# Three rounded passes for the fp32 input projection of a hybrid decoder step

## The reference, cut to what matters

```python
proj = xn @ w_in                       # 1024 -> 3*1024 + 1024 + 1536 + 16 columns
q, k, v, z, xbc, dt_raw = split(proj)
attn = rmsnorm(attend(rope(q), rope(k), v), g_attn)
xbc = silu(causal_conv(xbc))           # 4 taps
y, h = ssd_scan(x, dt, a, B, C, h0)    # h = h*exp(a*dt) + dt*x*B ;  y = C.h
y = rms(( y + d_skip*x) * silu(z)) * g_ssd
out = concat(attn, y) @ w_out          # then a PEER expert mixer
```

## Time and profile before

| | |
|---|---|
| device time, 3 runs | 1175.99, 1178.31, 1179.5 us |
| profiled execution: span | 1177.8 us (no other time of this execution is shown) |
| TensorE matmul busy | 1145.5 us, 97% |
| VectorE / ScalarE / GpSimd busy | 67% / 48% / 64% |
| mean granted TensorE clock | 0.994 of full speed |

### The profile page before, as it was taken

How to read it: one execution, slowest core, us unless ns; L and a number is a source line. 1 busy time by engine, 2 the same in 40 slices (tenths; PEclk the granted TensorE clock), 3 DMA queues, 4 the chain that set the end, 5 groups by cost and what they waited for, 6 DMA issues and landing times.

```text
span 1177.8 us, 24286 instructions
## 1 busy us (share of the span) xinstructions
PE 1145.5 (97%) x7599; PEld 1012.2 (86%) x7599; DVE 793.4 (67%) x1718; ACT 569.8 (48%) x1289; POOL 758.9 (64%) x642
## 2 busy tenths in 40 slices
PE   8999999989999999999999999999999999999997
PEld 7887777758888999999999999998888887888876
DVE  6789788874299997002899999984454466665534
ACT  3323223544354555565555554445555555555545
POOL 0066443237355998988666666676677797789754
PEclk9999999999999999999999999999999999999999
DMA  7468667695443666656544455545666697788653
GB/s 249 143 231 280 195 194 221 207 344 175 152 155 109 199 186 185 187 172 189 143 144 139 141 143 144 144 143 153 187 188 189 189 325 252 224 281 291 191 153 108
DMA packets 108667, 225.13 MB, mean 191 GB/s; under 512 B 12754, under 2 KB 21570, under 8 KB 108074
## 3 DMA queue, kind: packets, MB, share of 16 engines
q1 hardware_dynamic: 104706, 210.50, 57.5%
q0 software_dynamic: 2944, 10.49, 2.6%
q10 hardware_dynamic: 936, 3.14, 0.7%
HBM read 215.80 MB, written 8.19 MB: 190 GB/s over the span
## 4 chain that ended last, share of the span: by engine, by line
PE 71%; issue 1%; DVE 1%; POOL 0%; ACT 0%; DVEq 0%; POOLq 0%; ACTq 0%
PE bank L1689 31%; PE bank L1719 30%; PE bank L1699 5%; PE bank L1642 2%; PE bank L1654 1%; PE bank L1666 1%; DVE hl L2092 0%; PE bank L1739 0%; PE bank L1756 0%; POOL hl L1582 0%; DVE acts L2115 0%; PE bank L1747 0%; ACT acts L1925 0%; POOL hl L1567 0%; PE bank L1774 0%
## 5 line engine op out<-in xcount | busy, mean ns | idle before, releaser
L1567 POOL TENSOR_TENSOR hl<-ring,hl 128x512 fp32r<-128x512 f32 x448 | 585.5, 1317 | 187.5 <-ACT hl L1805 180.5
L1805 ACT CAST hl<-ring 128x512 fp32r<-128x512 f32 x512 | 317.1, 620 | 292.1 <-PE bank L1719 161.7
L1689 PE MATMUL bank<-split,hl 128*128 128x256 f32 x3072 | 378.5, 282 | 0.4 <-ACT hl L1805 0.3
L1689 PEld LDWEIGHTS bank<-split,hl 128*128 128x128 f32 x3072 | 366.3, 189 | 0.8 <-issue 0.5
L1719 PE MATMUL bank<-hl,split 128*128 128x512 f32 x1524 | 353.9, 394 | 1.9 <-DVE hl L2092 1.9
L1719 PEld LDWEIGHTS bank<-hl,split 128*128 128x128 f32 x1524 | 286.2, 188 | 69.7 <-DVE hl L2092 2.4
L533 PE MATMUL pj<-xn,ring 128*128 128x264 f32 x672 | 158.5, 392 | 0.7 <-ACT proj L824 0.7
L2085 DVE TENSOR_TENSOR split<-acts,split 128x256 fp32r<-128x256 f32 x128 | 128.3, 1028 | 40.0 <-ACT split L1901 37.0
L533 PEld LDWEIGHTS pj<-xn,ring 128*128 128x128 f32 x672 | 126.4, 192 | 24.7 <-issue 4.6
L2092 DVE TENSOR_TENSOR hl<-ring,hl 128x512 fp32r<-128x512 f32 x64 | 49.9, 779 | 115.6 <-ACT hl L1805 115.6
L2051 DVE TENSOR_SCALAR bv<-bkey,ig 128x130 f32<-128x130 f32 x256 | 86.0, 394 | 0.0
(11 more groups left out here) (369 smaller groups left out, 1107.1 us busy)
## 6 DMA issues: line engine op xcount, KB each, us to landing
ring<-in_uv SPq DMA_DIRECT2D x256, 256.0 KB, 2.7
ring<-in_v_rows SPq DMA_DIRECT2D x256, 256.0 KB, 3.1
ring<-in_w_ring SPq DMA_DIRECT2D x76, 512.0 KB, 4.2
room<-in_cache_k SPq DMA_DIRECT2D x64, 128.0 KB, 2.8
hs<-in_state_ssm SPq DMA_DIRECT2D x8, 512.0 KB, 4.7
out_ssm_s<-hs SPq DMA_DIRECT2D x8, 512.0 KB, 6.3
acts<-x_rows SPq DMA_DIRECT2D x8, 512.0 KB, 4.7
room<-in_cache_v SPq DMA_DIRECT2D x12, 256.0 KB, 5.7
```

Source lines behind the costliest of these rows:

```text
L1567: nc.gpsimd.tensor_tensor(hl[:, r % HL, 1], raw[:, r], hl[:, r % HL, 0].bitcast(F32), ALU.subtract).then_inc(lo_done, 1)
L1689: mm = nc.tensor.matmul(out, hl[:, r % HL, m, k * P:(k + 1) * P], split[:, x, kk, 0:TP], start=(kk == 0 and n == 0), stop=(kk == KD - 1 an ...
L1805: nc.scalar.copy(hl[:, r % HL, 0], raw[:, r]).then_inc(hi_done, 1)
```

## The change

Tiles 2 to 43 are computed in three passes of fp32r, like the output projection. For each half tile ScalarE rounds the weights into `wi` (`in_high`, right behind `copy(i-2)` in its queue), GpSimd writes the rest over the raw half in the ring (`in_low`), and TensorE runs 24 matmuls. `xn` is split once into `x_high` (ScalarE) and `x_low` (VectorE, which writes over `xn`). The room for `wi` and `x_high` comes from the state slots, which go from four to two, and some small tiles that move. From VectorE the first tap of tiles 4 to 11 (`tap`) and the scaling of the probabilities (`normal`) go to ScalarE; from GpSimd the decay of the state goes to ScalarE (`decay_state`, eight instructions of 128x128 per round). GpSimd's squares now start behind the last `in_low`; `values(0)` is issued in round 7 between two of its steps; `values(1)` moves to a later place of SyncE's queue, and its home from `hs` to the room of `x_high`. Waits on `hs_out` in the output stage become waits on `pj_copied`.

```diff
-HS, NS = 4, 6
+HS, NS = 2, 6
+HOMES = 4
@@ SyncE
-                    if n == 1:
-                        sp.wait_ge(ys_done, KD - 1)
-                        for s in (1, 2):
-                            sp.wait_ge(hs_out[s], 16 * (KD // HS))
-                    elif n == 2:
+                    if n in (1, 2):
                         sp.wait_ge(pj_copied, N_IN)
...
+                        if n == 0 and c >= HS:
+                            state(c)
-                        if n == 3 and 2 <= c < KD - HS + 2:
-                            state(c - 2 + HS)
...
-                            values(1)
...
                 tile(N_IN)
+                values(1)
                 values(2)
@@ GpSimd
+                def in_low(i):
+                    for a in range(2):
+                        n, r = 2 * (i - 2) + a, 2 * (i % RING) + a
+                        pool.wait_ge(w_hi, n + 1)
+                        nc.gpsimd.tensor_tensor(ring_lo[:, r], raw_o[:, r], wi[:, n % HL].bitcast(F32), ALU.subtract).then_inc(w_lo, 1)
+                for i in range(2, CONV_CH):
+                    in_low(i)
...
+                for c in range(KD):
+                    s, g = c % HS, c * GROUPS // KD
+                    in_low(CONV_CH + 4 * c)
...
+                    fed_in.then_inc(fed, 1)
+                    in_low(CONV_CH + 4 * c + 1)
+                    if c == KD - 1:
+                        values(0)
+                    pool.wait_ge(decayed, c + 1)
...
+                    sums.then_inc(st_done, 1)
+                    in_low(CONV_CH + 4 * c + 2)
+                    in_low(CONV_CH + 4 * c + 3)
@@ TensorE
+                    pe.wait_ge(pj_copied, i - 1)
+                    order = [(a, kind) for a in range(2) for kind in range(3)] if i > 2 else [(0, 0), (0, 2), (1, 0), (1, 2), (0, 1), (1, 1)]
+                    for n, (a, kind) in enumerate(order):
+                        half = 2 * (i - 2) + a
+                        if i == 2:
+                            pe.wait_ge(x_los if kind == 1 else x_his, a + 1)
+                        pe.wait_ge(w_lo if kind == 2 else w_hi, half + 1)
+                        for k in range(4):
+                            w = ring_lo[:, 2 * s + a, k * P:(k + 1) * P] if kind == 2 else wi[:, half % HL, k * P:(k + 1) * P]
+                            mm = nc.tensor.matmul(pj[i % 2][:, 0:NT], w, (x_low if kind == 1 else x_high)[:, 4 * a + k],
+                                                  start=(n == 0 and k == 0), stop=(n == 5 and k == 3))
@@ ScalarE
+                def in_high(i):
+                    act.wait_ge(ring_full[i % RING], 16 * (i // RING) + 16)
+                    for a in range(2):
+                        nc.scalar.copy(wi[:, (2 * (i - 2) + a) % HL], raw_o[:, 2 * (i % RING) + a]).then_inc(w_hi, 1)
+                in_high(2)
+                in_high(3)
+                def tap(i):
+                    act.wait_ge(pj_copied, i + 1)
+                    act.wait_ge(silu_done, i - 1)
+                    c = CT[i]
+                    nc.scalar.activation(cv[:, i % 2], proj[:, c, 0:TP], ACT.Copy, scale=par[:, P_CW + c * CONV_W + 3:P_CW + c * CONV_W + 4]
+                                         ).then_inc(tapped, 1)
                 def copy(i):
...
+                    if i + 2 < N_IN:
+                        in_high(i + 2)
...
+                for a in range(2):
+                    act.wait_ge(normed, a + 1)
+                    nc.scalar.copy(x_high[:, 4 * a:4 * a + 4], xn[:, 4 * a:4 * a + 4]).then_inc(x_his, 1)
                 copied_early(1)
...
+                def decay_state(c):
+                    s = c % HS
+                    act.wait_ge(hs_full[s], 16 * (c // HS) + 16)
+                    act.wait_ge(dds_done, 1)
+                    for b in range(NB):
+                        ins = nc.scalar.activation(hs[:, s, b], hs[:, s, b], ACT.Copy, scale=dds[:, c, 0, b:b + 1])
+                    ins.then_inc(decayed, 1)
+                def normal(c):
+                    for j in range(2):
+                        act.wait_ge(recips_done, 2 * c + j + 1)
+                        nc.scalar.activation(sc[:, j, 0:P], sc[:, j, 0:P], ACT.Copy, scale=stat[:, j, 4:5])
+                        nc.scalar.activation(sc[:, j, P:3 * P], sc[:, j, P:3 * P], ACT.Copy, scale=stat[:, j, 5:6]).then_inc(p_ready, 1)
...
                     copy(CONV_CH + 4 * c)
+                    if c:
+                        normal(c - 1)
                     decays(c)
...
                     copy(CONV_CH + 4 * c + 3)
+                    if c < KD - 1:
+                        decay_state(c + 1)
@@ VectorE
-                    link(nc.vector.tensor_scalar(to, proj[:, c, 0:TP], cw[3], None, ALU.mult))
+                    if i < 4:
+                        link(nc.vector.tensor_scalar(to, proj[:, c, 0:TP], cw[3], None, ALU.mult))
+                    else:
+                        dve.wait_ge(tapped, i - 3)
...
+                for half in range(2):
+                    k = slice(half * KD // 2, (half + 1) * KD // 2)
+                    dve.wait_ge(x_his, half + 1)
+                    nc.vector.tensor_tensor(x_low[:, k], xn[:, k], x_high[:, k].bitcast(F32), ALU.subtract).then_inc(x_los, 1)
                 conv(0)
```

111 lines of the change are left out of this document (55 added, 56 removed).

## The result

The changed kernel takes 1199.94 us (median of 4 runs, 1197.86 to 1202.91), the kernel before 1177.25 beside it. The ratio is 1.0201 [1.0173, 1.0229]: slower, by about 2%, outside the predicted range and beside the rival in which the memory port sets the pace (1200). The profiled span is 1201.1 us, 23.3 more than before; it belongs to the slowest of the four runs.

A forecast was written before the change was run, and what follows sets the result against it. TensorE was taken as the bound on average, with waits already costing 1.42 us a round. Rounds -11.6, opening +4.3, round 7 +2, output +2.5, clock +1 sum to -1.8: 1176.5 us, own range 1170 to 1183, full range 1162 to 1197.

The forecast's parts named there:

- The step that failed: Rounds 1 to 7: VectorE's waits grow to 5.7 us a round, about 18.4 us busy, within a 19.6 us round.
- the other two terms: The clock, +1 us, and the rest of the span from the first PEER matmul on, 0.
- The port rival: Rounds: VectorE and GpSimd never overlap on SBUF, a round needs 22.1 us; +22, 1200 us in all; chance 0.30.
- Its opening term (+7): Opening and round 0 in the case where the port sets the pace: 7 us later.
- TensorE's 0.65 us a tile: The 42 tiles: three passes start 2.92 us apart instead of 3.57, 27.3 us in all if everything else keeps up.
- The softmax chain: Rounds: ScalarE's scaling makes TensorE wait about 1.8 us at `turn_probs`; total waits 2.4 us a round instead of 1.42.
- Opening and round 0: Start to end of round 0: tile 5 and VectorE about 5 us late; +4.3 us, bounds +1 and +9.
- Round 7: `values(0)`'s four DMA issues, 4.6 us between GpSimd's steps, hold TensorE for about half: +2 us, between 0 and 4.
- Output stage: Its start: squares and `values(3)` issued later, value unit 3 to 7 us late; +2.5 us, between 0 and 5.
- State loads: Rounds: they wait longer for their slots but are issued a round ahead of the decay; no cost.
- Clock: Opening: more waits make one more half-speed stretch likely; +1 us, 0 to 4.

The follow-up runs named there:

- e16: e13's fp32 kernel plus 48 useless GpSimd subtractions in rounds 1 to 6, results read by nobody: 1178.94 us, 1.0027.
- e5: Changed kernel with GpSimd making only one of each tile's two low halves, used for both (a different computation): 1184.97 us, 1.0065.
- e18: e13's fp32 kernel plus 48 useless GpSimd subtractions and 48 useless ScalarE casts in rounds 1 to 6: 1180.02 us, 1.0037.
- e11: e10 with tiles 2 to 15 left in fp32, x split at the end of round 0, ScalarE copying tile 12 earlier: 1183.34 us, 1.0060.
- e2: Changed kernel with six useless fp32 matmuls on TensorE ahead of `turn_probs` in each round: 1198.43 us, 1.0197.
- e13: e11 with all tiles in fp32, no split of xn and no low weights, the smaller parts of the change kept: 1175.71 us, 1.0000.
- e1: Changed kernel with VectorE's softmax reciprocals ahead of `sample_out`: 1204.78 us, 1.0260.
- e4: Changed kernel with `evict_early(1)` ahead of the split of x and `conv(0)`, and `copy(3)` ahead of the exponentials: 1199.18 us, 1.0186.
- e3: Changed kernel with tile 13's low halves made before GpSimd's wait for `xdt`, tile 14's ahead of the state's sum: 1199.59 us, 1.0205.
- e8: Changed kernel with `values(0)` issued behind the last `in_low`, and `values(2)` ahead of `values(1)` on SyncE: 1202.30 us, 1.0208.
- e10: Changed kernel with `values(0)` and `values(3)` issued behind the last `in_low`, before the squares; SyncE's order unchanged: 1197.55 us, 1.0189.
- e7: Changed kernel with VectorE's order in a round made reciprocals, `ssd_in`, then `sample_out`: 1217.98 us, 1.0344.
- e9: Changed kernel with e7's order and SyncE's load of the next state issued two tiles later: 1225.19 us, 1.0423.
- e12: e11 with the order of e9 in the rounds: 1210.25 us, 1.0289.

## Why the prediction was wrong

**The step that failed** is "The waits grow with GpSimd's work: 114 us in seven rounds times 0.35 is 40 us, 5.7 a round, so about 18.4 us", taken to fit in a round of 19.6. The 0.35 was a mean over rounds in which GpSimd was idle for more than half of the time, taken as a price of added work. The first stretch of the earlier trace rows already spoke for more: (21.90 - 13.95) / (21.97 - 2.92) = 0.42 in a full round. Added work costs 0.52 to 0.55 (e16) and work taken out gives back 0.68 to 0.70 (e5). GpSimd's work came out longer too, 121 us for 114. VectorE was busy (141.15 - 4.4) / 7 = 19.5 us a round, and it has to wait 1.4 us for matmuls of its own chain: 20.9 us. Rounds 2 to 6 took 21.2. I had compared a busy time with a round's length as though it could be filled to the last, and gave nothing for those 1.4 us, which fall mostly on the rounds with key units.

In size, rounds 1 to 6 are 6.7 us of the 25.1 by which the sum missed the span. The largest part is the opening with round 0 (12.0 us), then round 7 (5.0) and the output stage (3.8); the other two terms missed by 2.3 the other way.

**The port rival had the mechanism and the total.** Its own sum for a round, 22.1 us "if no two overlap", is too high as a mean; the runs show about 21, and "whatever TensorE does" doesn't hold: rounds without key units take 20.4 us with fp32 tiles (e18) and 19.3 with three passes (e11). Its opening term (+7) was too small. That its total agrees with the measurement is partly chance: +5.9 for the seven rounds was +2.0 (-3.3 + 5.3).
The Trainium skill ("SBUF — State Buffer", SBUF: two separate sides) has a lock on a shared port pair, held for a whole instruction. The trace agrees on the turns: in round 0 four short instructions of VectorE took 3.66 us beside an unbroken row of GpSimd's. The rule gives neither the 0.52 nor the 5.04 us behind six instructions.

**TensorE's 0.65 us a tile** was right where nothing waits (2.90 us a tile), and the kernel could use it only in the rounds without key units: e2 shows that TensorE has spare time in rounds 2 to 6, and e18 against e11 that over five rounds the shorter tiles are worth nothing. In the kernel before, 5.6 us of rounds 2 to 6 were mostly TensorE's waits on VectorE and ScalarE, and e13 gets them (105.8 to 100.2) by the small moves alone. In the change these moves hid a part of the loss.

**The softmax chain.** Forecast was a wait of 1.8 us at `turn_probs`; it was 1.8 us (11.0 / 6). The reading of it, as the chain that decides, was wrong: e1 takes the wait away and e2 fills it, and neither gains more than 2 us.

**Opening and round 0**: +4.3 forecast (a choice; no sum leads from the 5 us to it), bounds +1 to +9, +16.3 measured. Two terms of it. Up to `expand(0)` +6.0, near the 5 us forecast for VectorE's arrears: tile 5 came at 39.70 (38 forecast), and the split of x took 4.57 us where I had 2.4 plus turns. The seven tiles' gain of 4.6 us didn't come, as VectorE's convolutions set the pace (a reading of the timeline; e4 agrees). Then round 0 lost 10.3 us for which the forecast had nothing ("round 0's own gain goes into waits on it"). Two things were missed. GpSimd waits 4.65 us for `xdt` with `in_low` of the next tiles behind it in its queue; I had not asked what stands behind that wait. And it then works without a pause from 77.56 on, just beside VectorE's chain to the last rope, which takes 18.0 us for 10.4: 7.6 of the 10.3 us. The chain's later start behind `expand(0)` is 3.2 more. e3 shows that the wait alone is not the cause. e5, with half of the low work, gives back 10.1 of the 16.4 us by the end of round 0; that the rest lies in ScalarE's casts and the split of x was not tried by itself.

**Round 7**: +2 forecast, bounds to 4. `values(0)` cost 5.5 us (e8). The 4.6 us of issues that I halved are not what TensorE waited for: the low halves came in time (no wait for them in the round). The loss is VectorE's shut-out of 5.04 us behind six instructions of GpSimd, which the issues had pushed to that place.

**Output stage**: +2.5 forecast, bounds to 5, +6.3 measured: 3.9 us before the first output tile and 2.3 in the output projection. The first comes mostly from a place that I had priced at nothing: "SyncE's `values(1)` ... stand within the same wait". `values(2)` stands behind it; its issues began 2.5 us behind the end of round 7, where they began 2.7 us ahead of it before, and TensorE waited 4.64 us for just that transfer. e8 and e10 show that three things end within a few microseconds of each other there (two transfers and VectorE's norms); each fix uncovers the next. What the 2.3 us are was not tried apart.

**State loads, "nothing"**: no wait on them shows in the rounds of the change as it stands; e7, e9 and e12 show that other orders run into them.

**Clock**: one more half-speed stretch was forecast; up to 341 us there were four before and there are about eleven. Their price in the rounds is about 2 us (e2); what they cost in the opening was not tried apart.
